# The scan's output with tokens on partitions: norm along the free axis, eight transposes back, scale and gate on the way out of PSUM

## The reference, cut to what matters

```python
o = _hgrn_direction(q, v, f_fwd, lb[0], False) + _hgrn_direction(q, v, f_bwd, lb[1], True)
o = rms_norm(o, o_gain.reshape(N_HGRN_HEADS, HGRN_VAL_DIM)).reshape(B, L, D_HGRN_V)
o = o * jax.nn.silu(gate)
return o.astype(h.dtype) @ w_out
```

## Time and profile before

| | us |
|---|---|
| median of 3 runs | 2833.17 (2829.45 to 2836.46) |
| the profiled execution, its own time | 2831.86 |
| its span in the profile | 2830.1 |
| TensorE busy | 2742.6 (97%) |
| VectorE busy | 1369.5 (48%) |
| ScalarE busy | 729.7 (26%) |
| GpSimd busy | 920.0 (33%) |

### The profile page before, as it was taken

How to read it: one execution, slowest core, us unless ns; L and a number is a source line. 1 busy time by engine, 2 the same in 40 slices (tenths; PEclk the granted TensorE clock), 3 DMA queues, 4 the chain that set the end, 5 groups by cost and what they waited for, 6 DMA issues and landing times.

```text
span 2830.1 us, 40126 instructions
## 1 busy us (share of the span) xinstructions
PE 2742.6 (97%) x16781; PEld 2467.6 (87%) x16781; DVE 1369.5 (48%) x1563; ACT 729.7 (26%) x1016; POOL 920.0 (33%) x403
## 2 busy tenths in 40 slices
PE   7998999999999999999999999999989999999998
PEld 6887998999999999999888888888868888888887
DVE  6287887442212322235777676778563223222234
ACT  3015887121100011003233334334231000110003
POOL 2230001334433444333322232224334344443441
PEclk9998999999999999999999999999999999999999
DMA  4010000111111111112111111112111111111111
GB/s 155 23 38 8 0 0 8 45 45 45 49 49 45 46 45 45 48 57 100 31 38 31 31 31 38 31 31 83 38 38 52 46 45 52 44 44 52 45 50 70
DMA packets 178223, 125.40 MB, mean 44 GB/s; under 512 B 4914, under 2 KB 171140, under 8 KB 178086
## 3 DMA queue, kind: packets, MB, share of 16 engines
q1 hardware_dynamic: 176790, 118.60, 13.8%
q10 hardware_dynamic: 1296, 4.73, 0.4%
HBM read 114.93 MB, written 8.39 MB: 44 GB/s over the span
## 4 chain that ended last, share of the span: by engine, by line
PE 86%; DVE 7%; issue 4%; ACT 3%; DMA 0%; ACTq 0%; SPq 0%; DVEq 0%
PE ps L1317 74%; PE ps L1443 3%; PE ps L1571 2%; PE ps L1536 1%; DVE ssq L884 1%; ACT prob L610 1%; PE ps L1393 1%; DVE tmp L892 1%; PE ps L1610 1%; ACT kk L705 1%; PE ps L1411 1%; PE ps L1548 0%; DVE y L959 0%; PE ps L1585 0%; DVE amax L1005 0%
## 5 line engine op out<-in xcount | busy, mean ns | idle before, releaser
L1317 PE MATMUL ps<-xh,wsp 128*128 128x512 f32 (+2 forms) x4864 | 1125.9, 356 | 17.3 <-DVE xl L878 12.7
L496 POOL TENSOR_TENSOR wsp<-raw,ones 128x1024 fp32r<-128x1024 f32 x198 | 379.7, 1918 | 1851.5 <-PE ps L1317 1832.9
L1317 PEld LDWEIGHTS ps<-xh,wsp 128*128 128x128 f32 x4864 | 839.7, 189 | 108.0 <-issue 21.3
L1317 PE MATMUL ps<-xl,wsp 128*128 128x348 f32 (+2 forms) x2432 | 617.1, 351 | 0.0
L1317 PE MATMUL ps<-ah,wsp 128*128 128x348 f32 (+2 forms) x2560 | 567.0, 350 | 0.0
L498 POOL TENSOR_TENSOR wsp<-raw,wsp 128x1024 fp32r<-128x1024 f32 x198 | 531.4, 2684 | 15.5
L1317 PEld LDWEIGHTS ps<-ah,wsp 128*128 128x128 f32 x2560 | 443.1, 188 | 44.7
L1317 PEld LDWEIGHTS ps<-xl,wsp 128*128 128x128 f32 x2432 | 430.4, 189 | 44.2
L655 ACT ACTIVATE tmp<-tmp 128x1044 f32<-128x1044 f32 (+1 forms) x64 | 68.5, 1070 | 1097.7 <-DVE tmp L1055 557.1
L1317 PE MATMUL ps<-al,wsp 128*128 128x348 f32 (+1 forms) x1280 | 322.5, 349 | 0.0
L1317 PEld LDWEIGHTS ps<-al,wsp 128*128 128x128 f32 x1280 | 225.2, 188 | 23.2
(11 more groups left out here) (199 smaller groups left out, 2799.5 us busy)
## 6 DMA issues: line engine op xcount, KB each, us to landing
raw<-in_w SPq DMA_DIRECT2D x128, 512.0 KB, 3.9
raw<-in_c_w_in SPq DMA_DIRECT2D x40, 512.0 KB, 3.8
raw<-in_ab_w_in SPq DMA_DIRECT2D x12, 512.0 KB, 3.8
xst<-in_x SPq DMA_DIRECT2D x8, 512.0 KB, 6.8
raw<-in_ab_w_out SPq DMA_DIRECT2D x8, 512.0 KB, 4.1
h_kept<-h ACTq DMA_DIRECT2D x8, 512.0 KB, 2.6
h<-h_kept SPq DMA_DIRECT2D x8, 512.0 KB, 5.9
out<-ost SPq DMA_DIRECT2D x16, 256.0 KB, 3.1
```

The lines of the kernel that those rows point to most:

```text
L496: nc.gpsimd.tensor_tensor(wsp[:, slot, 0, :], raw[:, slot, :], one, ALU.mult).then_inc(w_high, 1)
L1317: ins = M(ps[:, 3 * s + c, 0:n], w(a, k), b(k)[:, c0:c0 + n], start=(k == first and a == 0 and b is xa), stop=(k == last and a == 1))
```

## The change

The operands of the 23 output products swap sides, so that the output of a head comes out with tokens on partitions, 8 blocks of 128 tokens. ScalarE then squares each block out of PSUM with a sum along the free axis (8 instructions with an accumulator), and takes the root directly. VectorE inverts it and multiplies the PSUM banks by it on the way to `otk`. TensorE turns the 8 blocks back with transposes, into the same banks. VectorE applies the gain and the gate in one instruction per bank. `o_sum` and `o_bcast`, the copy to `tmp` and the separate gate multiply are gone. `o_gate` moves up in VectorE's order, to where `o_scale` was, and ScalarE's `gate_o` moves up to where `o_root` was. Part 3 now waits for `h_og`, the gated output.

```diff
-            def o_copy(hd):
-                if hd == 7:
-                    act.wait_ge(h_ol, 1)
-                elif hd:
-                    act.wait_ge(h_og, hd)
-                for r in range(2):
-                    act.wait_ge(h_o, 2 * hd + (r + 1))
-                    A(tmp[:, 0, N_META + 512 * r:N_META + 512 * (r + 1)], ps[:, spare(min(hd + 1, 7), r), :], ACT.Copy).then_inc(h_oe, 1)
-                act.wait_ge(h_oe, 2 * hd + 2)
-                A(sqo[:], tmp[:, 0, real], ACT.Square).then_inc(h_osq, 1)
-
-            def o_root(hd):
-                act.wait_ge(h_os, hd + 1)
-                A(stat[:, 0, 0:8], ps[:, spare(min(hd + 1, 7), 0), 0:8], ACT.Sqrt, bias=eps[:, :], scale=1.0 / P).then_inc(h_sd, 1)
+            def o_stats(hd):
+                for c in range(8):
+                    if c % 4 == 0:
+                        act.wait_ge(h_o, 2 * hd + (c // 4 + 1))
+                    A(junk[:, c, :], ps[:, spare(min(hd + 1, 7), c // 4), (c % 4) * P:(c % 4 + 1) * P], ACT.Square, accum_out=stat[:, 0, c:c + 1]).then_inc(h_osq, 1)
+                act.wait_ge(h_osq, 8 * hd + 8)
+                A(stat[:, 0, 0:8], stat[:, 0, 0:8], ACT.Sqrt, bias=eps[:, :], scale=1.0 / P).then_inc(h_sd, 1)
...
                 if prev:
-                    o_copy(hd - 1)
+                    o_stats(hd - 1)
                 pair_keys(hd, 4)
                 if prev:
-                    o_root(hd - 1)
+                    gate_o(hd - 1)
                 if nxt:
                     gate_f(hd + 1, 0, hg(hd, 0))
                     gate_f(hd + 1, 1, hg(hd, 1))
...
                 if nxt:
                     gate_q(hd + 1, hg(hd, 2))
-                if prev:
-                    gate_o(hd - 1)
...
-            def o_diag(hd):
+            def o_scale(hd):
                 dve.wait_ge(h_sd, hd + 1)
                 V.reciprocal(stat[:, 1, 0:8], stat[:, 0, 0:8]).then_inc(h_rs, 1)
                 dve.wait_ge(h_rs, hd + 1)
-                V.tensor_tensor(dgo[:], ident[:].rearrange("p (a b) -> p a b", a=1).to_broadcast([P, 8, P]),
-                                stat[:, 1, 0:8].rearrange("p (a b) -> p a b", b=1).to_broadcast([P, 8, P]), ALU.mult).then_inc(h_dg, 1)
-            def o_scale(hd):
                 for r in range(2):
-                    dve.wait_ge(h_bc, 2 * hd + (r + 1))
-                    V.scalar_tensor_tensor(t, t, small[:, OG + hd:OG + hd + 1], ps[:, spare(min(hd + 1, 7), r), :], ALU.mult, ALU.mult).then_inc(h_bm, 1)
+                    scale = stat[:, 1, 4 * r:4 * r + 4].rearrange("p (a b) -> p a b", b=1).to_broadcast([P, 4, P])
+                    V.tensor_tensor(otk[:, 4 * r:4 * r + 4, :], ps[:, spare(min(hd + 1, 7), r), :].rearrange("p (a b) -> p a b", b=P), scale, ALU.mult).then_inc(h_bm, 1)
 
             def o_gate(hd):
...
-                V.tensor_tensor(dst, tmp[:, 0, real], zq[:, real] if hd == 7 else tmp[:, 1, real], ALU.mult).then_inc(h_og, 1)
+                for r in range(2):
+                    half = slice(N_META + 512 * r, N_META + 512 * (r + 1))
+                    dve.wait_ge(h_ot, 2 * hd + (r + 1))
+                    V.scalar_tensor_tensor(h[:, hd, half] if hd < KEPT else tmp[:, 0, half], ps[:, spare(min(hd + 1, 7), r), :], small[:, OG + hd:OG + hd + 1],
+                                           zq[:, half] if hd == 7 else tmp[:, 1, half], ALU.mult, ALU.mult).then_inc(h_og, 1)
...
                 if prev:
-                    o_diag(hd - 1)
+                    o_scale(hd - 1)
                 merge(hd, 4)
                 join_queries(hd, 4)
                 join_keys(hd, 5)
                 if prev:
-                    o_scale(hd - 1)
+                    o_gate(hd - 1)
                 if not nxt:
                     first_add(0)
                 merge(hd, 5)
                 join_queries(hd, 5)
                 join_keys(hd, 6)
                 if nxt:
                     store_real(zq[:], hg(hd, 2))
-                if prev:
-                    o_gate(hd - 1)
                 merge(hd, 6)
...
-                        parts = [(vt[:, c, :], aas[hd % 2][:, c - 1, :]), (st[:, c - 1, :], qqs[hd % 2][:, 1, t0:t0 + n])]
+                        parts = [(aas[hd % 2][:, c - 1, :], vt[:, c, :]), (qqs[hd % 2][:, 1, t0:t0 + n], st[:, c - 1, :])]
...
-            def o_sum(hd):
-                pe.wait_ge(h_osq, hd + 1)
-                for i in range(8):
-                    ins = M(ps[:, spare(min(hd + 1, 7), 0), i:i + 1], sqo[:, i * P:(i + 1) * P], ones[:, 0:1], start=True, stop=True)
-                ins.then_inc(h_os, 1)
-
-            def o_bcast(hd):
-                pe.wait_ge(h_dg, hd + 1)
-                for r in range(2):
-                    M(ps[:, spare(min(hd + 1, 7), r), :], ones[:], dgo[:, 4 * r:4 * r + 4, :].rearrange("p a b -> p (a b)"),
-                      start=True, stop=True).then_inc(h_bc, 1)
+            def o_turn(hd):
+                for r in range(2):
+                    pe.wait_ge(h_bm, 2 * hd + (r + 1))
+                    for a in range(4):
+                        ins = nc.tensor.transpose(ps[:, spare(min(hd + 1, 7), r), a * P:(a + 1) * P], otk[:, 4 * r + a, :], ident[:])
+                    ins.then_inc(h_ot, 1)
...
-                part(hg(hd, 2), hx, lx, KT, REAL, {1: [o[1]], 3: [lev[4]], 5: [o[2]], 7: [lev[5]]})
+                part(hg(hd, 2), hx, lx, KT, REAL, {3: [lev[4]], 5: [o[1]], 7: [lev[5]]})
                 if hd:
-                    pe.wait_ge(h_bm, 2 * hd)
+                    pe.wait_ge(h_og, 2 * hd)
...
-            between = ({1: [lambda: o_sum(6)], 3: [lev[4]], 5: [lambda: o_bcast(6)]},
+            between = ({3: [lev[4]], 5: [lambda: o_turn(6)]},
...
-                       {1: [lambda: o_sum(7)], 4: [lambda: o_bcast(7)]},
+                       {4: [lambda: o_turn(7)]},
```

More of the change, by code:

```diff
@@ L157, in encoder @@
         ktb = at("ktb", [P, 7, P], F32, o_k + 4096)
-        sqo = at("sqo", [P, SEQ], F32, o_k)
-        dgo = at("dgo", [P, 8, P], F32, o_k + 4096)
+        otk = at("otk", [P, 8, P], F32, o_k)
+        junk = at("junk", [P, 8, P], F32, o_k + 4096)
         oh7 = at("oh7", [P, SEQ], F32R, o_k)
@@ L282, in encoder @@
         h_o = sem("o_ready")
-        h_oe = sem("o_copied")
-        h_osq = sem("o_squared")
-        h_os = sem("o_sums")
+        h_osq = sem("o_square_sums")
         h_sd = sem("o_root")
         h_rs = sem("o_inverse")
-        h_dg = sem("o_diagonal")
-        h_bc = sem("o_norm_broadcast")
         h_bm = sem("o_normed")
+        h_ot = sem("o_turned")
         h_og = sem("o_gated")
@@ L817, in _ @@
                 head(hd)
-            act.wait_ge(h_og, 7)
+            act.wait_ge(h_og, 14)
             A(oh6[:], tmp[:, 0, real], ACT.Copy).then_inc(h_oh, 1)
-            o_copy(7)
-            o_root(7)
-            act.wait_ge(h_og, 8)
+            o_stats(7)
+            act.wait_ge(h_og, 16)
             A(oh7[:], tmp[:, 0, real], ACT.Copy).then_inc(h_oh, 1)
@@ L1171, in o_diag @@
                 dve.wait_ge(h_rs, hd + 1)
-                V.tensor_tensor(dgo[:], ident[:].rearrange("p (a b) -> p a b", a=1).to_broadcast([P, 8, P]),
-                                stat[:, 1, 0:8].rearrange("p (a b) -> p a b", b=1).to_broadcast([P, 8, P]), ALU.mult).then_inc(h_dg, 1)
-            def o_scale(hd):
                 for r in range(2):
-                    dve.wait_ge(h_bc, 2 * hd + (r + 1))
-                    t = tmp[:, 0, N_META + 512 * r:N_META + 512 * (r + 1)]
-                    V.scalar_tensor_tensor(t, t, small[:, OG + hd:OG + hd + 1], ps[:, spare(min(hd + 1, 7), r), :], ALU.mult, ALU.mult).then_inc(h_bm, 1)
+                    scale = stat[:, 1, 4 * r:4 * r + 4].rearrange("p (a b) -> p a b", b=1).to_broadcast([P, 4, P])
+                    V.tensor_tensor(otk[:, 4 * r:4 * r + 4, :], ps[:, spare(min(hd + 1, 7), r), :].rearrange("p (a b) -> p a b", b=P), scale, ALU.mult).then_inc(h_bm, 1)
             def o_gate(hd):
-                dve.wait_ge(h_bm, 2 * hd + 2)
+                if hd == 7:
+                    dve.wait_ge(h_oh, 1)
                 dve.wait_ge(h_gt, hd + 1)
-                dst = h[:, hd, real] if hd < KEPT else tmp[:, 0, real]
-                V.tensor_tensor(dst, tmp[:, 0, real], zq[:, real] if hd == 7 else tmp[:, 1, real], ALU.mult).then_inc(h_og, 1)
+                for r in range(2):
[3 more added lines that the diff above has]
+                                           zq[:, half] if hd == 7 else tmp[:, 1, half], ALU.mult, ALU.mult).then_inc(h_og, 1)
             def first_add(k):
@@ L1258, in _ @@
             dve.wait_ge(h_oh, 1)
+            dve.wait_ge(h_og, 14)
             V.tensor_tensor(ol6[:], tmp[:, 0, real], oh6[:], ALU.subtract).then_inc(h_ol, 1)
@@ L1263, in _ @@
             first_add(5)
-            o_diag(7)
             o_scale(7)
@@ L1267, in _ @@
             dve.wait_ge(h_oh, 2)
+            dve.wait_ge(h_og, 16)
             V.tensor_tensor(ol7[:], tmp[:, 0, real], oh7[:], ALU.subtract).then_inc(h_ol, 1)
@@ L1531, in o_products @@
```

(6 more changed lines are left out.)

## The result

| | before | after |
|---|---|---|
| median, us | 2831.55 (4 runs, 2829.45 to 2836.46) | 2809.12 (4 runs, 2807.76 to 2809.96) |
| profiled execution, its own time | 2831.86 | 2808.71 |
| its span | 2830.1 | 2806.6 |

The ratio is 0.9922, with a 95% interval of 0.9907 to 0.9937. The median moved by 22.4 us and the profiled span by 23.5. The forecast was 2809.0 and a gain of 24.2. It started from the median of three runs of the kernel before, 2833.17; the fourth run brought that median to 2831.55, so the start was 1.6 too high and the gain 1.8 too large. That the two cancel to within 0.1 us of the measured time is luck; the gain is what was forecast, and it came out at 22.4 by the medians and 23.5 in the profiled span.

The account below looks back on a forecast made before the run. TensorE, busy 97%, bounds the kernel. Gains 20.5 (six heads) + 1.1 (output of head 6) + 2.6 (head 7) = 24.2 us take the profiled 2831.86 to 2807.7; with 1.3 for the runs' median, 2809.0; range 2803 to 2819.

Parts of the forecast that it names:

- `o_sum`, 1.77: On TensorE ahead of level 4: removing the sums saves 1.68 us plus 0.09 for one change of stream less.
- `o_bcast` against the transposes, 0.85, less 0.15 of a new wait: On TensorE: 1.72 us gives way to eight transposes at 0.87; the second four wait 0.15 for VectorE's second multiply.
- Level 7, 0.95: TensorE's wait before each head's last level goes, as VectorE's join_queries(6) no longer comes late: 0.95 us per head.
- Six heads: Heads 1 to 6, making the outputs of heads 0 to 5: gain 3.42 us each, 20.5 together.
- Output of head 6: Made in head 7, where VectorE is last: removing the sums gains nothing, earlier transposes gain 1.1 us.
- Output of head 7: `o_sum` and `o_bcast` stand on TensorE's chain: gain 1.77 + 0.85 = 2.6 us.
- ScalarE: Ahead of level 4: squares with accumulator at 0.47 us each, six more table loads, 3 us of cover, no cost.
- The gate before part 3: TensorE's new wait for the gated output before part 3 costs nothing: gate done at 1724.15, cover 0.84 us.
- Dear transposes: Rival: transposes on TensorE cost their recorded length, 1.3 us more each time; gain 13.7, 2819.5 us; chance 0.07.
- Squares: Rival: ScalarE's accumulating squares delay level 4 from 1.0 us each; at 1.5 us slower, 2837 us; chance 0.04.
- The late gate: Rival: the gated output comes late before part 3; with 3 us delay, gain near 11, 2822 us; chance 0.07.
- Collisions between VectorE and GpSimd: Rival: they keep the wait before level 7 or move it to level 6 or part 3; 2814.7 us; chance 0.15.

Follow-up runs that it names:

- sums_back: Changed kernel with eight products of the squares against a column of ones put back on TensorE, results unread; 2823.12 us, ratio 0.9975 to before.
- scale_first: Changed kernel with VectorE's inverse and scaling moved ahead of its store of the next head's backward decay gate; 2808.83 us, ratio 0.9926 to before.
- order_only: Kernel before, arithmetic untouched, with ScalarE's silu right behind the root and VectorE's gate multiply right behind the scaling; 2822.93 us, ratio 0.9975.
- turns_twice: Changed kernel with each of an output's eight transposes issued twice into the same place; 2811.17 us, ratio 0.9931 to before.

## Why the prediction was right, point by point

- **The path.** TensorE was the path and stayed it. Of the 24.2 us forecast the stage shows 603.74 - 580.22 = 23.5. A head takes 80.25 us from output to output where it took 83.5; 80.1 was forecast.
- **`o_sum`, 1.77.** From `o_products` to level 4: 1716.43 - 1701.26 = 15.17 before (its start, 1701.26, from the same chain as the earlier trace rows), 1703.81 - 1690.42 = 13.39 after. 1.78.
- **`o_bcast` against the transposes, 0.85, less 0.15 of a new wait.** From level 4 to level 5: 8.55 before, 8.06 after, so 0.49 and not 0.70. This is the one term of the sum that was clearly mis-sized, and it takes 1.3 us off the six heads. The wait was seen, for the second half only, but it is 0.37 (1.24 against 0.87): the data of a transpose is its weight load, and in the timeline of PEld both halves' loads stand still for VectorE instead of running ahead under the products. sums_back and scale_first each give the 0.37 back.
- **Level 7, 0.95.** From level 5 to level 7: 14.90 before, 13.92 after: 0.98. order_only shows that it is the order's. VectorE ends the second multiply of `join_queries(6)` at 1723.40, 2.4 us ahead of level 7 (1.9 was worked out).
- **Six heads:** 20.5 forecast, 501.13 - 481.50 = 19.6 measured. **Output of head 6:** 1.1 forecast, 1.24 measured; sums_back puts the cost of its sums at 0.05, the nothing that was forecast. The waits ahead of level 4 there are 0.9, in the large products for VectorE's `xl`, and 1.7 before the level itself, 2.6 together; the forecast had 2.8, all of it before the level. **Output of head 7:** 2.6 forecast, 2.65 measured.
- **ScalarE.** The size was off, to the safe side. Squares of 0.28 and reads of 0.21 overlap, four of each take 1.14 us, 0.29 a block and not 0.47, and the keys are done 4.4 us ahead of level 4, not 3. The six added table loads are there (35 in the whole execution, 29 before) and cost TensorE nothing. Its timeline in the changed kernel (compare):

```profile
1695.59 0.28 ACT L709 ACTIVATE junk<-ps 128x128 f32<-128x128 f32 x1 [1.31 <-PE ps L1524]
...
1696.36 0.29 ACT L709 ACTIVATE junk<-ps 128x128 f32<-128x128 f32 x1
1696.51 0.22 ACT L709 ACTIVATION_READ_ACCUMULATOR junk<-ps 128x1 f32 x1
1696.75 1.28 ACT L711 ACT_TABLE_LOAD   x1
1698.05 0.30 ACT L711 ACTIVATE stat<-stat,eps 128x8 f32<-128x8 f32 x1
1698.25 1.14 ACT L728 ACTIVATE kp<-kk 128x512 f32<-128x512 f32 x2
```

- **The gate before part 3.** No wait there, as forecast. VectorE's lines in the changed kernel (compare): the scaling at 1.29 a pair, the gate at the 1.40 of L1179, done at 1713.25, part 3 reached at 1712.95 + 1.40 = 1714.35. Cover 1.1, forecast 0.84.

```profile
1707.07 1.29 DVE L1163 TENSOR_TENSOR otk<-ps,stat 128x512 f32<-128x512 f32 x2
...
1711.85 1.40 DVE L1173 SCALAR_TENSOR_TENSOR h<-ps,small,tmp 128x512 f32<-128x512 f32 x2
```

- **The rivals.** Dear transposes: refuted by turns_twice. Squares: their threshold lies where it was put, and the real squares are far under it. The late gate: real as a mechanism, priced by two runs, not reached by this change; a listed wait of 0.56 us cost 0.84, and one of 6.7 us cost 8.5, most of the excess there by the clock. Collisions between VectorE and GpSimd: they stand in the kernel before and in the changed one (L1137 at 1717.00 takes 2.84), but none of them costs TensorE a wait before levels 5 to 7; scale_first ran into one that does, in head 7.

## What to carry to other kernels

Price a removed instruction by how far it moves the chain, and then look at what TensorE now reaches earlier: of 1.77 us freed here, 0.37 went into waiting for the next operand. When a change both removes work and reorders, run the order alone: here it was 6.1 of 23.5 us, and the same arithmetic at the old places lost 28 us against the kernel before. Where a producer sits behind an unrelated store on its engine, moving it ahead can pay (0.385 us a head here), but check the stages with another rhythm, where a shift of 0.2 us can put a GpSimd instruction on top of two VectorE ones.

## What the runs showed of the hardware that I had not expected

- A transpose that waits for its data costs more than a glance at the multiplies that feed it suggests: its weight load (a record of 0.14 us) waits too and no longer runs ahead. Eight took 0.87 with the data there and 1.22 to 1.25 with it just coming.
- A wait of 6.7 us made a head 8.5 us longer: the granted clock was 0.50 at its end and 0.71 on the mean over the 6.3 us behind it, and 1.73 us were lost there each time. Behind waits of 0.56, 0.62 and 1.7 us nothing of this kind shows: the granted clock stays at 1.00, levels keep 1.08 us from start to start, and only the three products right behind the wait of 0.56 were 0.10 longer.
- VectorE's multiplies with both operands in SBUF ended some 0.55 us after a GpSimd instruction, at 2.40 and 2.88 us instead of 0.69 and 0.68, while a store out of PSUM in the same company kept its length. In the changed kernel such a store and the split beside it are this pair, VectorE's and GpSimd's:

```profile
1728.59 1.25 DVE L1082 TENSOR_TENSOR zi<-ps,rms 128x1044 f32<-128x1044 f32 x1 [3.48 <-PE ps L1305]
```

```profile
1728.80 1.90 POOL L493 TENSOR_TENSOR wsp<-raw,ones 128x1024 fp32r<-128x1024 f32 x1 [9.51 <-PE ps L1305]
```
